# Hybrid decoder trunk: the convolution's gated input transposed by VectorE and moved through device memory

## The reference, cut to what matters

```python
z = h @ w_in
c_q, c_kv, k_r, u_conv, u_pool, gate_logits = jnp.split(z, split_at, axis=-1)
def conv_branch(u, conv_w, conv_b, ln_g, ln_b, w_out):
    a, g = jnp.split(u, 2, axis=-1)
    h = a * jax.nn.sigmoid(g)
    h = lax.conv_general_dilated(h, conv_w[:, None, :], window_strides=(1,),
                                 padding=[(CONV_WIDTH - 1, 0)], ...,
                                 feature_group_count=CONV_CHANNELS) + conv_b
    h = jax.nn.silu(layer_norm(h, ln_g, ln_b))
    return h @ w_out
```

## Time and profile before

| what | value |
|---|---|
| median of 3 runs | 785.55 us (785.39 to 786.66) |
| the profiled execution's own time | 785.48 us |
| its span, first to last instruction | 783.6 us |
| granted TensorE clock, mean | 0.998 |
| TensorE (PE) busy | 775.5 us, 99% of the span |
| VectorE (DVE) busy | 573.1 us, 73% |
| ScalarE (ACT) busy | 422.0 us, 54% |
| GpSimd (POOL) busy | 95.7 us, 12% |

### The profile page before, as it was taken

One profiled execution on the slowest core, in us unless ns is written; L12 is line 12 of the kernel. 1 busy time (PEld: TensorE's weight loads), 2 busy tenths in 40 slices (PEclk: granted clock), 3 DMA queues, 4 the chain that ended last, 5 costly groups with the idle time before them and its releaser, 6 DMA issues.

```text
span 783.6 us, 10189 instructions
## 1 busy us (share of the span) xinstructions
PE 775.5 (99%) x3702; PEld 654.7 (84%) x3702; DVE 573.1 (73%) x827; ACT 422.0 (54%) x597; POOL 95.7 (12%) x147
## 2 busy tenths in 40 slices
PE   9999999999999999999999999999999999999997
PEld 7998888888888888888889888888888888888885
DVE  6689999789675666654476999996887665557553
ACT  6587565654554454454475666565536544445441
POOL 2524000222300000000221230002304000000000
PEclk9999999999999999999999999999999999999999
DMA  9677445545567666676355684445564766666741
GB/s 358 237 249 228 170 161 161 162 160 187 180 220 238 198 213 223 214 240 208 126 202 161 230 251 148 161 162 161 171 224 143 246 210 218 212 202 223 231 137 54
DMA packets 53456, 154.39 MB, mean 197 GB/s; under 512 B 10544, under 2 KB 15664, under 8 KB 53408
## 3 DMA queue, kind: packets, MB, share of 16 engines
q1 hardware_dynamic: 51856, 149.72, 57.6%
q0 software_dynamic: 1408, 3.52, 1.6%
q10 hardware_dynamic: 144, 0.52, 0.2%
HBM read 143.77 MB, written 1.05 MB: 185 GB/s over the span
## 4 chain that ended last, share of the span: by engine, by line
PE 98%; DMA 1%; DVE 0%; ACT 0%; issue 0%; DVEq 0%; POOLq 0%; SPq 0%; POOL 0%; ACTq 0%
PE acc L463 28%; PE acc L465 28%; PE acc L464 28%; PE acc L562 7%; PE tp L537 2%; PE misc L758 1%; PE tp L776 1%; PE tp L549 1%; DMA gates<-x_cols 1%; PE tp L740 0%; PE misc L463 0%; PE misc L465 0%; PE misc L464 0%; PE misc L725 0%; PE misc L727 0%; PE misc L789 0%
## 5 line engine op out<-in xcount | busy, mean ns | idle before, releaser
L1228 DVE TENSOR_TENSOR w_lo<-raw,w_hi 128x1024 fp32r<-128x1024 f32 (+2 forms) x245 | 297.7, 1226 | 120.1 <-ACT w_hi L894 119.6
L894 ACT ACTIVATE w_hi<-raw 128x1024 fp32r<-128x1024 f32 (+2 forms) x251 | 257.2, 1039 | 161.9 <-PE acc L465 155.0
L463 PE MATMUL acc<-w_hi,xT_hi 128*128 128x512 f32 (+2 forms) x692 | 268.2, 388 | 0.0
L465 PE MATMUL acc<-w_hi,xT_lo 128*128 128x512 f32 (+2 forms) x692 | 265.2, 383 | 0.0
L464 PE MATMUL acc<-w_lo,xT_hi 128*128 128x512 f32 (+2 forms) x692 | 264.8, 383 | 0.0
L465 PEld LDWEIGHTS acc<-w_hi,xT_lo 128*128 128x128 f32 x692 | 130.0, 188 | 24.7
L464 PEld LDWEIGHTS acc<-w_lo,xT_hi 128*128 128x128 f32 x692 | 130.1, 188 | 24.0
L463 PEld LDWEIGHTS acc<-w_hi,xT_hi 128*128 128x128 f32 x692 | 130.1, 188 | 23.7
L463 PE MATMUL acc<-w_hi,hT_hi 128*128 128x512 f32 (+1 forms) x300 | 117.3, 391 | 0.0
L465 PE MATMUL acc<-w_hi,hT_lo 128*128 128x512 f32 (+1 forms) x300 | 116.3, 388 | 0.0
L464 PE MATMUL acc<-w_lo,hT_hi 128*128 128x512 f32 (+1 forms) x300 | 116.2, 387 | 0.0
(11 more groups left out here) (150 smaller groups left out, 639.8 us busy)
## 6 DMA issues: line engine op xcount, KB each, us to landing
raw<-weights SPq DMA_DIRECT2D x247, 512.0 KB, 3.8
raw<-weights SPq DMA_DIRECT2D x14, 384.0 KB, 3.6
gates<-gates SPq DMA_DIRECT2D x160, 32.0 KB, 2.5
raw<-weights SPq DMA_DIRECT2D x8, 288.0 KB, 4.2
gain<-gains SPq DMA_DIRECT2D x4, 512.0 KB, 6.6
qk<-gates POOLq DMA_DIRECT2D x18, 64.0 KB, 3.5
x_sb<-x_rows SPq DMA_DIRECT2D x2, 512.0 KB, 9.3
out_rows<-x_sb SPq DMA_DIRECT2D x4, 256.0 KB, 2.0
```

The lines of the kernel that those rows point to most:

```text
L463: pe.matmul(out, a_hi, b_hi, start=start, stop=False)
L465: return pe.matmul(out, a_lo, b_hi, start=False, stop=stop)
L894: ins = act.activation(w_hi[:, s, first:end], raw[:, s, first:end], ACT.Copy, scale=by)
L1228: ins = dve.tensor_tensor(w_lo[:, s, 0:width], raw[:, s, 0:width], f(w_hi[:, s, 0:width]), ALU.subtract)
```

## The change

TensorE's eight transposes of `hc` and their two uses of `tp` are taken out. VectorE transposes `hc` itself, in 32 x 32 blocks within each quadrant of partitions, into `turned_h` (two instructions of 128 x 512, right behind the two that write `hc`). SyncE stores all of `turned_h`, 512 KB, to a new buffer in device memory with one DMA (`blocks_out`, behind the load of unit 16), and loads it back with four DMAs of 128 KB, one for each quadrant of 32 partitions (`blocks_in`, behind the load of unit 18, waiting for the store to have landed). Both stand in SyncE's one queue among the weight loads. ScalarE copies `placed_h` to `hcT` with two instructions, now behind CQ's copy out of PSUM and ahead of hi(16), and waits for the four loads there.

On VectorE the taps before unit 17's low part go: `los(11, 17)` stands in one piece. They begin with `taps(3)` behind lo(17), with three behind each of lo(18) to lo(21) instead of two, none behind lo(26) instead of two, two behind each of lo(27) and lo(28) instead of five. In the gate loop it is four up to i = 7 and five from i = 8 on. Counting 124 out, 30 are issued ahead of the loop (45 before), 62 by the end of i = 7, 122 by the end of i = 19, and the last two come in i = 20.

```diff
+        turned_h, placed_h = (gates[:, i, 0:TOK * CONV] for i in range(2))
...
+        between_h = nc.dram_tensor("between_h", (QUADS, P, TOK * P), F32, kind="Internal").ap()
...
+        def h_blocks(buf, t):
+            return buf.rearrange("p (q t k j) -> p q t k j", q=QUADS, t=TOK, k=CT)[:, :, t, :, :].rearrange(
+                "p q k j -> p k q j")
...
+            def blocks_out(between, turned, ready, count, out):
+                sp.wait_ge(ready, count)
+                sp.dma_start(between.rearrange("q p m -> p q m"),
+                             turned.rearrange("p (q m) -> p q m", q=QUADS)).then_inc(out, 16)
+            def blocks_in(between, placed, out, count, landed):
+                sp.wait_ge(out, 16 * count)
+                for q in range(QUADS):
+                    sp.dma_start(placed[BLK * q:BLK * (q + 1), :].rearrange("f (a m) -> f a m", a=QUADS),
+                                 between[q].rearrange("(a f) m -> f a m", a=QUADS)).then_inc(landed, 16)
...
+                    if u == U_Q:
+                        blocks_out(between_h, turned_h, h_turned, TOK * (l + 1), h_out)
+                    if u == U_Q + 2:
+                        blocks_in(between_h, placed_h, h_out, l + 1, h_in)
...
-                def hc_transposes(i):
-                    if i == 1:
-                        if l == 0:
-                            pe.wait_ge(const_in, 16)
-                        for t in range(TOK):
-                            acc_freed(pe, l, 2 + t, "A")
-                            transposes(TPN["HC0"] + t, [(hc[:, t, c * P:(c + 1) * P], P) for c in range(CT)])
-                col_group(U_CQ, 4, 2, Q_RANK, 0, "CQ", XT, beside=hc_transposes)
+                col_group(U_CQ, 4, 2, Q_RANK, 0, "CQ", XT)
...
-                his(8, 12)
-                if l == 0:
-                    act.wait_ge(pad_zero, 1)
-                for t in range(TOK):
-                    n = TPN["HC0"] + t
-                    tp_filled(act, l, n)
-                    act.activation(hcT[...], split3(tp[:, n % 2, :], CT), ACT.Copy).then_inc(tp_free[n % 2], 1)
-                his(12, 16)
+                his(8, 16)
                 for t in range(TOK):
                     bank(t, "CQ")
                     act.activation(cq[...], acc[...], ACT.Copy, scale=rstd(l, R_X + t)).then_inc(free[t], 1)
+                act.wait_ge(h_in, 16 * QUADS * (l + 1))
+                for t in range(TOK):
+                    dst = hcT[:, :, TAPS - 1 + t * P:TAPS - 1 + (t + 1) * P]
+                    act.activation(dst.rearrange("p k (q j) -> p k q j", q=QUADS), h_blocks(placed_h, t), ACT.Copy
+                                   ).then_inc(h_stored, 1)
                 his(16, 17)
...
-                los(11, 12)
-                for t in range(TOK):
-                    tp_emptied(dve, l, TPN["HC0"] + t)
-                taps(4)
-                los(12, 13)
-                taps(3)
-                for u in range(13, 16):
-                    lo(u)
-                    taps(2)
-                los(16, 17)
+                for t in range(TOK):
+                    acc_freed(dve, l, 2 + t, "A")
+                    dve.transpose(h_blocks(turned_h, t), hc[:, t, :].rearrange("p (k q j) -> p k q j", k=CT, q=QUADS)
+                                  ).then_inc(h_turned, 1)
+                los(11, 17)
                 for t in range(TOK):
                     lo_T(f"CQ{t}", ...)
+                dve.wait_ge(h_stored, TOK * (l + 1))
                 los(17, 18)
-                taps(1)
+                taps(3)
                 for u in range(18, 22):
                     lo(u)
-                    taps(2)
+                    taps(3)
...
                 los(26, 27)
-                taps(2)
                 for u in range(27, 29):
                     lo(u)
-                    taps(5)
+                    taps(2)
...
-                    taps(4)
+                    taps(4 if i < 8 else 5)
```

More of the change, by code:

```diff
@@ L89, in fulls @@
     return len([u for u in upto if pair == 0 or u not in WIDE])
-TP = (["X0", "X1", "X2", "X3", "HC0", "HC1", "CQ0", "CQ1", "CKV0", "CKV1",
+TP = (["X0", "X1", "X2", "X3", "CQ0", "CQ1", "CKV0", "CKV1",
        "MT0", "MT1", *(f"{piece}{n}" for n in range(8) for piece in "PV"), "O0", "O1",
@@ L282, in build @@
         k_nope = sem("k_nope")
+        h_turned = sem("h_turned")
+        h_out = sem("h_out")
+        h_in = sem("h_in")
+        h_stored = sem("h_stored")
         q_turned = sem("q_turned")
@@ L672, in _, with cq_transposes @@
                 col_group(U_A, 4, 2, 512, 1, "A", XT, begun=1 if l else 0)
-                def hc_transposes(i):
-                    if i == 1:
+                col_group(U_CQ, 4, 2, Q_RANK, 0, "CQ", XT)
+                def cq_transposes(i):
+                    if i == 2:
                         if l == 0:
                             pe.wait_ge(const_in, 16)
-                        for t in range(TOK):
-                            acc_freed(pe, l, 2 + t, "A")
-                            transposes(TPN["HC0"] + t, [(hc[:, t, c * P:(c + 1) * P], P) for c in range(CT)])
-                col_group(U_CQ, 4, 2, Q_RANK, 0, "CQ", XT, beside=hc_transposes)
-                def cq_transposes(i):
-                    if i == 2:
                         for t in range(TOK):
@@ L983, in _ @@
                 act.preload_act_table(ACT.Tanh if l else ACT.Sin)
-                his(8, 12)
-                if l == 0:
-                    act.wait_ge(pad_zero, 1)
-                for t in range(TOK):
-                    n = TPN["HC0"] + t
-                    tp_filled(act, l, n)
-                    act.activation(hcT[:, :, TAPS - 1 + t * P:TAPS - 1 + (t + 1) * P],
-                                   split3(tp[:, n % 2, :], CT), ACT.Copy).then_inc(tp_free[n % 2], 1)
-                his(12, 16)
+                his(8, 16)
                 for t in range(TOK):
@@ L996, in _ @@
                                    scale=rstd(l, R_X + t)).then_inc(free[t], 1)
+                if l == 0:
+                    act.wait_ge(pad_zero, 1)
+                act.wait_ge(h_in, 16 * QUADS * (l + 1))
[3 more added lines that the diff above has]
+                                   ).then_inc(h_stored, 1)
                 if l == 0:
@@ L1347, in _ @@
                                              in1=sg[:, t, :], op0=ALU.mult, op1=ALU.mult).then_inc(free[2 + t], 1)
-                los(11, 12)
                 for t in range(TOK):
-                    tp_emptied(dve, l, TPN["HC0"] + t)
+                    acc_freed(dve, l, 2 + t, "A")
[3 more added lines that the diff above has]
+                for t in range(TOK):
+                    lo_T(f"CQ{t}", hT_lo[:, H_CQ:H_CQ + 3, tokens(t)], hT_hi[:, H_CQ:H_CQ + 3, tokens(t)])
+                dve.wait_ge(h_stored, TOK * (l + 1))
                 if l == 0:
                     dve.wait_ge(par_in, 16)
-                taps(4)
-                los(12, 13)
+                los(17, 18)
                 taps(3)
-                for u in range(13, 16):
-                    lo(u)
-                    taps(2)
-                los(16, 17)
-                for t in range(TOK):
-                    lo_T(f"CQ{t}", hT_lo[:, H_CQ:H_CQ + 3, tokens(t)], hT_hi[:, H_CQ:H_CQ + 3, tokens(t)])
-                los(17, 18)
-                taps(1)
                 for u in range(18, 22):
                     lo(u)
-                    taps(2)
+                    taps(3)
                 for t in range(TOK):
```

## The result

| | before | after |
|---|---|---|
| median of 4 runs each, on one chip | 785.63 us | 805.95 us (805.51 to 806.92) |
| ratio, 95% interval | | 1.0263 (1.0251 to 1.0275) |
| span of the profiled execution | 783.6 us | 803.7 us |
| TensorE (PE) busy | 775.5 us | 780.3 us |

What follows compares the result with a forecast made beforehand. TensorE was taken to bound the kernel (98% of the span). Lateness at the mean, 1.1 + d in layer 0 and 1.8 + d in layer 1 with d = 2.8, gave 8.5 on 785.48: 794.0 us, range 787.4 to 798.5.

Steps and rivals of the forecast that it cites:

- h that comes late: ScalarE's copies to hcT wait for the trip through memory; all of h back at 41.5 us against 38.7.
- taps that come late: VectorE, full over the gates, owes 11 more taps, 4.35 us; the last two stand behind step 20's work.
- 149.2 + d: Forecast time in us of layer 0's last tap on VectorE, against 143.99 before.
- d: How much later than 38.7 us h is back for ScalarE's copies; taken as 2.8 us (0 to 5.2).
- GpSimd's sum ends 2.5 us after it: Sum of the taps ends 2.5 us after the last tap, as before: at 151.7 + d in layer 0.
- the row of 2.38 us: Profile row for lo(49)'s two halves on VectorE in the kernel before; read as containing waits, priced at 1.3 us.
- the price of step 20: Gate step 20's work on VectorE through the last two taps: division, lo(49), lo_T and taps, 3.0 us.
- 8.5: Total forecast loss in us over both layers: 1.1 + 1.8 + 2 x 2.8, added to 785.48.
- a longer trip: Rival: store and loads back share engines badly with units 17 and 18; d 4 or more, 796.5 up; chance 0.13.
- H in time, taps late: Rival: h back by 38.7, d = 0, only the taps' tail left: 788.4 us; chance 0.12.
- It cancels: Rival: TensorE's time saved, with the tap tail half as long as worked out: 785 to 787 us; chance 0.10.
- no wait at all: Rival: TensorE never waits and gains 2 x 0.87 us: 783.7 us; chance 0.08.

Runs made afterwards that it cites:

- the kernel without the trip: Changed kernel without the store and loads back; ScalarE copies straight from VectorE's quadrant transposes, so the convolution's input is in wrong places: 797.69 us.
- the order alone: Kernel before, transposes still on TensorE, with only the changed kernel's places for the taps: 797.75 us, ratio 1.0160.
- the filled wait: Changed kernel with 18 unused matmuls of 512 columns on TensorE ahead of its wait for the channel sum: 802.52 us.
- the kernel with the taps moved and the trip hidden: Changed kernel, copies behind hi(19), 14 taps instead of 20 ahead of the queries' transposes, 12 instead of 4 around units 26 to 28: 788.56 us.
- three attempts: On the kernel with the taps moved: low parts held at i = 19, 790.46 us; norm steps one place later, 790.62; that plus taps shifted, 790.09.

## Why the prediction was right in direction and wrong in size

**Right.** Both mechanisms of the forecast, h that comes late and taps that come late, bind. The last tap came where "149.2 + d" puts it: 149.2 + 4.2 = 153.4, measured 153.32; in the kernel without the trip, at about d = 0, the addition starts at 149.38. The transposes' 2 x 0.87 us were spent before the mean. The store went out at 33.2 where I had 33.3.

**The step that failed** is the sentence "GpSimd's sum ends 2.5 us after it", with what I had read into the row of 2.38 us, that it "contains" waits of VectorE for others. The row was the evidence of a hold-up: the pair ran beside GpSimd's additions. I took it out of the price of step 20 (rightly, 1.41 against my 1.3) and did not ask what happens when the low parts come first. In the new order the last two taps stand directly ahead of four scaled low parts, and the addition waits for all of them: 3.69 us instead of 1.28, with the sum done 4.57 us after the last tap. Shown from four sides: the addition is 3.69 us with the order alone, 1.27 when the low parts are held back, 1.28 when it starts first and the pair then takes 2.94, and the pair is 1.41 in the kernel before when it is held back. The Trainium skill, "SBUF — State Buffer", section "SBUF: two separate sides", states such a rule: where VectorE's instruction has two inputs in SBUF and GpSimd's reads SBUF, the one that starts first keeps the other out until it has ended. The scaled low parts read `raw` and `w_hi`, the addition reads `cacc`, and the traces agree; they add that the addition waited for a train of four instructions, not for one. What follows the train, the low part made from `tp` in PSUM and `hT_hi`, took its usual 0.69 us and did not keep the addition out any longer, which ended 1.1 us behind the train.

**The term left out** is the clock. The forecast took TensorE's wait at its length. A wait of 4.47 us was followed by 5.4 us at a granted clock of 0.59, and the filled wait shows 1.7 to 2.0 us a layer for it.

**The term mis-sized** is d: 4.2 and not 2.8. The store, at "36.9", landed at 37.8 (4.7 us behind a load, 3.5 without one), the issue of the four loads was shorter than 0.6 each (1.75 in all), and the last one took 3.7 us instead of 2.7 (issued at 39.16, landed by 42.85). The fit that I weighed from the Trainium skill, "DMA: Bandwidth & Descriptors", section on the anatomy of one DMA, gave 40.7 for h back (and 792.4 in the sum, not 792.3); the measured 42.9 does not agree with it.

The sum with the measured terms: 8.5 + 2 x 1.4 (d) + 2 x 2.1 (sum of the taps: 4.57 less 2.5) + 2 x 1.7 (clock) = 18.9 of the 20.3 us between the medians; with the clock at 2 x 2.0 it is 19.5 of the 20.0 us between the profiled executions. The remaining 0.5 to 1.4 us are not assigned to a term. TensorE's waits on the way to the mean fell out differently from what I had written, without entering the sum: 1.9 us at Q in each layer where I had "a little", 1.2 at unit 23's low part where I had "more", and none at the scores.

**Of the rivals,** "a longer trip" had d right, and its 796.5 and up was still too low by the other two terms. "H in time, taps late" has its case in the run without the trip (d of 0.2), which took 797.69 us and not 788.4: it lacks the same two terms. "It cancels" and "no wait at all" are excluded: the order alone costs 12.3 us. What stays open is why the kernel with the taps moved and the trip hidden keeps 3 us: its own waits at mean and variance are 2.1 us, and three attempts to remove them made it slower.

## What to carry to other kernels

A hand-off from one engine to another is to be priced with what the first engine does next: if VectorE goes on with instructions that read two SBUF tensors, GpSimd's sum behind it can take three times as long, and a row that is longer than its siblings on one side is the sign of it. A wait of TensorE costs its length and, behind each of 2.27 us or more that I looked at in the layers, a stretch at the lower clock; look at the clock column and the count of matmuls behind each wait. Here a change that gave the bound engine 0.9 us a layer moved 4 us a layer of the next engine's work into a stretch where that engine had nothing to spare, and it lost.

## What the runs showed of the hardware

- VectorE's `scalar_tensor_tensor` 128 x 512 with both tensors in SBUF against GpSimd's `tensor_tensor` 128 x 512 out of SBUF: whichever starts second is held up, 1.28 to 3.69 us on GpSimd, 1.41 to 2.38 or 2.94 us for VectorE's pair.
- Granted clock over the 5.4 us behind a standstill of TensorE in a full-clock stretch: 1.00 after 0.99 us and after 1.90 us, 0.68 after 2.27 us, 0.70 after 2.5 us, 0.50 after 4.24 us, 0.59 after 4.47 us.
- 512 KB from SBUF to device memory in pieces of 1 KB took 4.7 us behind a weight load of 384 KB and 3.5 us without it; four loads back of 128 KB each were all there 5.1 us after the first was issued in the one case and 6.2 us in the other.
